# First FFN of a streaming-encoder layer: the running sum over the remaining modulation in PSUM, its pieces and loads in another order

## What is computed

```python
c_act = jax.nn.silu(c)
mod = c_act @ w_ada[layer] + b_ada[layer]            # 1024 x 9216, in fp32
(sh1, sc1, gt1, sh2, sc2, gt2, sh3, sc3, gt3) = jnp.split(mod, N_MOD, axis=-1)
h = modulate(rms_normalize(x), sh1, sc1)
x = x + 0.5 * gt1[:, None, :] * swiglu(h, w_ffn1_in[layer], w_ffn1_out[layer])
...
def swiglu(h, w_in, w_out):
    g, u = jnp.split(h @ w_in, 2, axis=-1)
    return (jax.nn.silu(g) * u) @ w_out
```

## Time and profile before

| | |
|---|---|
| time, median of 3 runs | 2207.29 us (2206.86 to 2210.01) |
| profiled execution, own time | 2208.98 us |
| its span, first to last instruction | 2207.3 us |
| mean granted clock of TensorE | 0.939 |
| busy: PE / DVE / POOL / ACT | 91% / 54% / 42% / 34% |

### The profile page before, as it was taken

How to read it: one execution, slowest core, us unless ns; L and a number is a source line. 1 busy time by engine, 2 the same in 40 slices (tenths; PEclk the granted TensorE clock), 3 DMA queues, 4 the chain that set the end, 5 groups by cost and what they waited for, 6 DMA issues and landing times. The chain is left out here.

```text
span 2207.3 us, 25592 instructions
## 1 busy us (share of the span) xinstructions
PE 2016.5 (91%) x9248; PEld 1663.3 (75%) x9248; DVE 1202.8 (54%) x1745; ACT 757.7 (34%) x1359; POOL 921.5 (42%) x643
## 2 busy tenths in 40 slices
PE   3698999989999969999999899698799999999997
PEld 3577777777888848888888777576588888888886
DVE  5775566663587761223441455644744435347777
ACT  5422222222344431324441234423433323234444
POOL 5786677776000051000001111326888878750002
PEclk8798999999999979679999999898899999999999
DMA  7145445541786310111100110132123233239662
GB/s 294 59 153 165 151 152 184 159 158 49 263 296 204 105 41 20 39 39 39 38 20 20 58 39 29 51 112 95 59 101 115 96 105 108 79 106 372 205 195 91
DMA packets 204613, 257.10 MB, mean 116 GB/s; under 512 B 14014, under 2 KB 124882, under 8 KB 202962
## 3 DMA queue, kind: packets, MB, share of 16 engines
q1 hardware_dynamic: 204498, 255.59, 34.7%
HBM read 206.71 MB, written 48.84 MB: 116 GB/s over the span
## 5 line engine op out<-in xcount | busy, mean ns | idle before, releaser
L372 POOL TENSOR_TENSOR ffn_ring_b_lo<-ffn_raw_in,ffn_ring_b_hi 128x512 fp32r<-128x512 f32 x176 | 261.8, 1496 | 129.5 <-ACT ffn_ring_b_hi L367 129.5
L1473 POOL TENSOR_TENSOR mx_w_lo<-mx_raw_w,mx_w_hi 128x1024 fp32r<-128x1024 f32 x32 | 79.5, 2494 | 439.5 <-ACT mx_w_hi L1289 439.4
L784 PE MATMUL bank<-ffn_w_hi,ffn_a_hi 128*128 128x512 f32 x616 | 240.5, 390 | 1.2 <-DVE ffn_w_lo L768 1.2
L786 PE MATMUL bank<-ffn_w_hi,ffn_a_lo 128*128 128x512 f32 x616 | 240.0, 390 | 0.0
L785 PE MATMUL bank<-ffn_w_lo,ffn_a_hi 128*128 128x512 f32 x616 | 239.9, 389 | 0.0
L1194 PE MATMUL bank<-h_hi,ffn_ring_a_hi 128*128 128x512 f32 x352 | 150.6, 428 | 73.1 <-ACT ffn_g L950 49.5
L367 ACT CAST ffn_ring_b_hi<-ffn_raw_in 128x512 fp32r<-128x512 f32 x176 | 108.8, 620 | 297.0 <-PE bank L1196 282.7
L110 POOL TENSOR_SCALAR rms<-rms 128x1 f32<-128x1 f32 x24 | 16.1, 670 | 456.7 <-ACT ffn_junk L104 430.7
L757 ACT CAST ffn_a_hi<-ffn_a_stage 128x512 fp32r<-128x512 f32 x154 | 95.6, 621 | 201.4 <-PE bank L786 197.0
L1024 DVE TENSOR_TENSOR ffn_u<-bank,ffn_u 128x512 f32<-128x512 f32 x110 | 75.7, 688 | 145.1 <-PE bank L1196 145.1
L1194 PE MATMUL bank<-h_hi,ffn_ring_b_hi 128*128 128x512 f32 x352 | 140.8, 400 | 9.1 <-issue 5.3
(11 more groups left out here) (303 smaller groups left out, 4963.7 us busy)
## 6 DMA issues: line engine op xcount, KB each, us to landing
ffn_raw_in<-in_w_ffn_in SPq DMA_DIRECT2D x88, 512.0 KB, 6.1
ffn_a_stage<-hidden SPq DMA_DIRECT2D x154, 256.0 KB, 3.5
ffn_w_stage<-in_w_ffn_out SPq DMA_DIRECT2D x132, 256.0 KB, 3.2
ada_rest<-in_w_ada SPq DMA_DIRECT2D x64, 448.0 KB, 4.0
hidden<-ffn_u SPq DMA_DIRECT2D x88, 256.0 KB, 2.0
hidden<-ffn_g SPq DMA_DIRECT2D x66, 256.0 KB, 2.0
mx_raw_w<-in_w_mix_in SPq DMA_DIRECT2D x28, 512.0 KB, 3.8
ada_ring<-in_w_ada SPq DMA_DIRECT2D x8, 1024.0 KB, 12.0
```

The lines of the kernel that those rows point to most:

```text
L372: pool.tensor_tensor(self.lo(q), self.source(b, m), self.hi(q).bitcast(F32), ALU.subtract)\
L784: pe.matmul(dst, a_hi, w_hi, start=first, stop=False, skip_group_check=True)
L786: mm = pe.matmul(dst, a_lo, w_hi, start=False, stop=True, skip_group_check=True)
L1473: pool.tensor_tensor(lo, raw_w[:, slot, :], hi.bitcast(F32), ALU.subtract).then_inc(w_lo_done[slot], 1)
```

## The change

The running sum moves from SBUF to PSUM: it takes banks 6 and 7, columns 0 to 895 of the two, for pieces 0 to 6; piece 7 reads it there and writes the final sum to `rest_acc` in SBUF, where TensorE reads it as before. The results of TensorE's 7 matmuls move to columns 384 to 390 of bank 7. Piece 0 also waits for `rest_kept`. In VectorE's order piece 1 moves up behind piece 0, pieces 4 and 5 behind the `hidden` that they preceded (5 behind `sums123` as well), pieces 6 and 7 behind `hidden` (a12) and `sum4`. In SP's order the loads are spread otherwise around the stores.

```diff
@@ -612,17 +612,18 @@
                        bias=self.mcol[:, r:r + 1]).then_inc((self.h_b12, self.h_b22)[half], 1)
 
     def dve_rest(self, dve, b, k):
+
         c = self.c.KD * (b - 1) + k
         dve.wait_ge(self.rest_loaded[c % 2], 16 * (c // 2) + 16)
-        c_k = self.c_act[:, k:k + 1]
+        c_k, acc = self.c_act[:, k:k + 1], self.c.bank[:, 6:8, :].rearrange("p b n -> p (b n)")[:, 0:self.COLS]
         if k == 0:
             if b > 1:
                 dve.wait_ge(self.rest_ready, b - 1)
-            dve.tensor_scalar(self.rest_acc, self.rest_piece[c % 2], c_k, None, ALU.mult)\
-                .then_inc(self.rest_summed, 1)
+                dve.wait_ge(self.rest_kept, b - 1)
+            dve.tensor_scalar(acc, self.rest_piece[c % 2], c_k, None, ALU.mult).then_inc(self.rest_summed, 1)
         else:
             dve.wait_ge(self.rest_summed, c)
-            dve.scalar_tensor_tensor(self.rest_acc, self.rest_piece[c % 2], c_k, self.rest_acc,
+            dve.scalar_tensor_tensor(self.rest_acc if k == self.c.KD - 1 else acc, self.rest_piece[c % 2], c_k, acc,
                                      ALU.mult, ALU.add).then_inc(self.rest_summed, 1)
 
     def pe_rest(self, pe, b):
@@ -630,14 +631,14 @@
         if b > 1:
             pe.wait_ge(self.rest_kept, b - 1)
         for r in range(self.TILES):
-            mm = pe.matmul(self.c.bank[:, 6, r:r + 1], self.rest_acc[:, r * P:(r + 1) * P], self.ones[:, :],
+            mm = pe.matmul(self.c.bank[:, 7, BANK - P + r:BANK - P + r + 1], self.rest_acc[:, r * P:(r + 1) * P], self.ones[:, :],
                            start=True, stop=True)
         mm.then_inc(self.rest_ready, 1)
 
     def dve_rest_kept(self, dve, b):
         at = slice((b - 1) * self.TILES + 2 * self.c.KD, b * self.TILES + 2 * self.c.KD)
         dve.wait_ge(self.rest_ready, b)
-        dve.tensor_tensor(self.mcol[:, at], self.c.bank[:, 6, 0:self.TILES], self.bcol[:, at], ALU.add)\
+        dve.tensor_tensor(self.mcol[:, at], self.c.bank[:, 7, BANK - P:BANK - P + self.TILES], self.bcol[:, at], ALU.add)\
             .then_inc(self.rest_kept, 1)
 
     def dve_finish(self, dve):
@@ -859,18 +860,17 @@
             for b in range(STEPS):
                 rest = start and 1 <= b <= start.STEPS
                 if rest:
-                    for k in range(3):
-                        start.load_rest(sp, b, k)
+                    start.load_rest(sp, b, 0)
+                    start.load_rest(sp, b, 1)
                 store(b, "a11")
                 if rest:
-                    start.load_rest(sp, b, 3)
-                    start.load_rest(sp, b, 4)
+                    for k in range(2, 6):
+                        start.load_rest(sp, b, k)
                 if b + 2 < STEPS:
                     sp.wait_ge(weights.lo_done, N * (b + 1))
                     weights.load(sp, b + 2)
                 if rest:
-                    for k in range(5, KD):
-                        start.load_rest(sp, b, k)
+                    start.load_rest(sp, b, 6)
                 if start and b == start.STEPS + 1:
                     start.store_rows(sp)
                 if b == LAST:
@@ -879,7 +879,10 @@
                         fo.load_a(sp, n)
                         if n < 3:
                             fo.load_w(sp, n)
-                store(b, "a22", "s1", "s2", "s3", "a12", "s4")
+                store(b, "a22")
+                if rest:
+                    start.load_rest(sp, b, 7)
+                store(b, "s1", "s2", "s3", "a12", "s4")
             for a in fo_operands:
                 sp.wait_ge(spilled[a], 16 * STEPS)
             sp.wait_ge(p_ready, N * STEPS)
@@ -1095,12 +1098,12 @@
                     if b > 1:
                         start.dve_rest_kept(dve, b - 1)
                     start.dve_rest(dve, b, 0)
+                    start.dve_rest(dve, b, 1)
                 make_u2(b, 0)
                 make_u2(b, 1)
                 if b == 0:
                     halved.cut_lo(dve, "t4")
                 if rest:
-                    start.dve_rest(dve, b, 1)
                     start.dve_rest(dve, b, 2)
                 make_u3(b, 0)
                 make_u3(b, 1)
@@ -1110,24 +1113,24 @@
                     start.dve_rows(dve)
                 make_c22(b, 0)
                 make_c22(b, 1)
+                hidden(b, U3, U3, 1, c22_made, made["a22"])
                 if rest:
                     start.dve_rest(dve, b, 4)
-                hidden(b, U3, U3, 1, c22_made, made["a22"])
                 make_c12(b, 0)
                 make_c12(b, 1)
+                hidden(b, U2, U2, 2, c12_made, a21_made)
+                sums123(b)
                 if rest:
                     start.dve_rest(dve, b, 5)
-                hidden(b, U2, U2, 2, c12_made, a21_made)
-                sums123(b)
                 make_c21(b, 0)
                 if b == LAST:
                     fo.cut_lo(dve, 0)
                 make_c21(b, 1)
+                hidden(b, S1, C11, 3, c21_made, made["a12"])
+                sum4(b)
                 if rest:
                     start.dve_rest(dve, b, 6)
                     start.dve_rest(dve, b, 7)
-                hidden(b, S1, C11, 3, c21_made, made["a12"])
-                sum4(b)
             for n in range(1, len(fo.items)):
                 fo.sum_w(dve, n + 1)
                 fo.cut_lo(dve, n)
```

## The result

The changed kernel took 2144.21 us (median of four runs: 2121.54, 2137.68, 2150.74, 2151.32), the kernel before beside it 2207.07 us (2206.61 to 2210.01). It is faster, and the median lies 0.3 us from the forecast of 2144.5. But four runs that spread over 30 us are not what was forecast, and the lowest lies 20 us under the range. So the median alone says little; the trace has to tell where the time went. Its run took 2121.54 us, with a span of 2119.8.

A forecast was written before the change was run, and what follows sets the result against it. TensorE bounds the kernel, with time to win only where it stands still or runs slow: 63.6 us in the first FFN. Less 0.8 us of remaining stall, 2207.29 - 62.8 = 2144.5 us, range 2142 to 2157.

The forecast's parts named there:

- What can be won: First FFN, eight steps: 378.9 us could become 315.3, winning 39.5 us of TensorE standing still and 24 of slow clock.
- (1): First FFN, VectorE: `hidden` and `sum4` before pieces 6 and 7 take 4.2 us out of the copy's way.
- (2): First FFN, VectorE: with pieces 4 and 5 moved, one piece (5) remains on the path to `make_c21`.
- (3): First FFN, VectorE: a piece with its sum in PSUM takes 1.1 us, 1.03 of it on the path.
- rival C: First FFN: pieces in PSUM still wait for GpSimd, stall 1.8 us, clock may fall, 2180 us; chance 8%.
- (4): First FFN, TensorE's wait for the copy: 0.1 us per step stays, no clock lost, cost 0.8 us in all.
- (5): First FFN, SP's queue: loads in the new order among the stores cost nothing.
- (6): First FFN, VectorE: the added wait on `rest_kept` is for its own instruction right before and costs nothing.
- B: First FFN: GpSimd slows `hidden`, a stall of about 1 us per step stays, 2152.5 us; chance 15%.
- D: First FFN: VectorE's writes to banks 6 and 7 hold up TensorE, 70 us lost, 2214.5 us; chance 4%.
- E: First FFN: pieces in PSUM run so slowly (3.9 us each) that VectorE fills the step, no change; chance 3%.
- the sum: Whole kernel: 63.6 us won less 0.8 given back, from the median 2207.29 to 2144.5 us.

The follow-up runs named there:

- PSUM alone: Running sum moved to PSUM with the order of before kept, against the kernel before: 2150.27 us, ratio 0.9774.
- 2 us later: Nine idle matmuls added between the first FFN's input and output products: in the change 2122.93 us, in the kernel before 2212.06 us.

## Why the prediction was right, and where it was wrong

**What can be won, 63.6 us in the first FFN: right.** In the traces the eight steps went from 378.9 to 318.0, by 60.9 us against 62.8 forecast, and with piece 5 moved once more to 315.75, by 63.2. Standing still and slow clock went together.

**(1), (2) `hidden` and `sum4` first, pieces 4 and 5 elsewhere: right.** Undoing all of the order leaves 18.9 us of waits (PSUM alone), and the one move of pieces 6 and 7 makes 37.7 of the order's 48.5 us in the eight steps.

**(3) The sum in PSUM: right, size off by 0.05.** I took 1.1 us; it was 1.142 to 1.158 in all 64 pieces, beside a busy GpSimd or not. The rival C fell: a scalar pointer from SBUF beside one SBUF input does not make the instruction wait. Of the 120 against 58 fixed cycles that the Trainium skill gives ("VectorE: DVE Perf Modes", TRN2 errata) nothing shows: 1.144 was the fastest piece from SBUF alone and 1.142 the fastest from PSUM. Its rule on who interferes with whom ("SBUF — State Buffer") is borne out, and the scalar does not count as an input. Piece 0 took 1.154 instead of 0.97, 0.2 worse and hidden, as said.

**(4) What is left of the stall: the size was off.** I wrote 0.1 us per step; the eight steps have (318.0 - 315.3) / 8 = 0.34. In the timeline `make_c21(b, 0)` starts at 237.10, 2.70 before the product was due (239.57 + 0.227 = 239.80); in the earlier trace rows it was 542.18 - 538.29 = 3.89. It came 1.19 later, where I had x = 1.03: the piece holds VectorE for 1.05 (236.05 to 237.10), the other 0.14 were already there ahead of it, the "tenth or two" that I named and did not add. With a slack of 1.0 that is the stall of 0.2, and another 0.1 went in the matmul start behind it. No clock was lost, as forecast.

**(5), (6) Loads and the added wait: nothing, right.** With piece 5 moved, 39.67 us per step are all busy, so no load was late.

**Rivals.** B (a slow `hidden` behind `make_c21`) did not come: 0.69 us in all eight steps. With pieces 6 and 7 alone moved it came in seven of eight. D and E fell: matmuls under pieces keep 0.39 in the rows and 0.227 apart.

**What failed is the step "the sum":** 2207.29 - 62.8 assumes that all that stands behind the first FFN keeps its time. It did not: in the profiled run 28.4 us went in the attention stage, and 3.5 came in others. The trace of before held the warning, a stretch of 65 us at clock 0.50 in a stage whose start the change moves by 60 us; I looked for the slow clock only inside the first FFN. Where the clock fell there, the stage did not keep its time either: 266.1 us against 262.9, and the gain was 59.1 us instead of 62.8 (60.8 in the eight steps and 1.2 before them, less 3.2 in the stage). So the range, 2142 to 2157, stood around one of two values: with the clock low in the stage the change is at 2149 to 2151, with it high at 2121. The median of four, 2144.21, lies between by the mixture of its runs, and that it meets the forecast is chance. A range that took the stage in would have reached down to 2207.3 - 62.8 - 28.4 = 2116. Why the stage's clock falls in some runs and not in others stays open.

## What to carry to other kernels

A clock that falls in a stage can come or go by an edit hundreds of microseconds earlier. Before a gain is summed up, list every stretch of the kernel at half clock, also the ones that the edit doesn't touch, and put each into the range; when the runs of one kernel fall into two groups, compare stage by stage, not by medians. Where a short pause precedes a stage of short matmuls, a few idle matmuls are a cheap trial (here 28.9 us for 1.4 us of work), but in each version anew, since in one of these it did nothing. And of several delays that end in the same wait each edit looks good alone: 48 to 49 us by the order and 30.2 by PSUM, 60.2 together.

## What was not expected of the hardware

The granted clock in the attention stage has two outcomes for nearly the same work: 234.5 us at 1.00, or 263 to 266 with 65 to 72 us at 0.50. Small edits elsewhere change how often each one comes: the change as it is had the lower time in one of nine runs (and 2137.7, between the two, in another), 2 us later and on another chip in five of five; the kernel before had a low clock in ten of eleven runs when 2 us later, and in all 15 without that on the same chip. The Trainium skill ("TensorE: Matmul & The Clock Gate", Part 1) has the moment of a change of clock vary with the phase of a counter that runs on its own. That one and the same kernel comes out both ways agrees with it; that the unaltered kernel before came out low in every run does not look like a free phase, and no run here decides it. Once low it stayed so for all of the short matmuls of the first part and came back with the dense ones.

VectorE's scalar_tensor_tensor of 128x896 fp32 takes the same 1.14 to 1.16 us whether it reads its sum from PSUM and writes there or writes to SBUF (1.146 to 1.149), while in SBUF throughout it took 1.144 to 2.230.
